# Moving four side steps in the schedule of a one-core hybrid decoder layer

## What is computed

```python
u = rmsnorm(h, g_pre)
p = u @ w_in                       # 4096 x (12*1024 + 8)
log_f = log_sigmoid(f_logit + b_forget)            # the 8 extra columns, one per FoX head
o_fox = forgetting_attention(fq, fk, fv, log_f) * silu(fgate)
o_sb  = stick_breaking_attention(sq, sk, sv) * silu(sgate)
o_ssm = s5_mixer(su, ...) * silu(ssm_gate)         # complex diagonal scan, gelu, GLU
o_lru = rglru_mixer(lx, ...) * silu(lru_gate)      # conv4, block gates, scan
out = h + rmsnorm(concatenate([o_fox, o_sb, o_ssm, o_lru]) @ w_out, g_post)
```

## Time and profile before

| | |
|---|---|
| Median of 3 runs | 1551.7 us (1551.67 to 1552.07) |
| The profiled execution | 1551.9 us |
| Its span, first to last instruction | 1550.0 us |
| Granted TensorE clock, mean | 0.997 |
| PE matmul busy | 1525.6 us (98%), 7090 recorded |
| DVE busy | 927.1 us (60%) |
| ACT busy | 858.8 us (55%) |
| POOL busy | 86.6 us (6%) |
| Mean transfer rate | 188 GB/s |

### The profile page before, as it was taken

The page is one execution under the profiler, slowest core; times in us unless marked ns, Lnnn a source line. Parts: engine busy times, 40 slices in busy tenths (PEclk is TensorE's granted clock), DMA queues, the critical chain, the costliest instruction groups (busy, mean ns, idle before and its releaser), DMA issues.

```text
span 1550.0 us, 22156 instructions
## 1 busy us (share of the span) xinstructions
PE 1525.6 (98%) x7090; PEld 1254.7 (81%) x7090; DVE 927.1 (60%) x1154; ACT 858.8 (55%) x1158; POOL 86.6 (6%) x130
## 2 busy tenths in 40 slices
PE   8999999999999999999999999999999999999996
PEld 7888887778877788888878888888888888888885
DVE  6544478899888895454554544455566444444445
ACT  6644476666776656566554445556666443444442
POOL 0000010111211110000000000000000000000000
PEclk9999999999999999999999999999999999999999
DMA  8466656665665665565655555555556866666675
GB/s 303 136 198 190 188 167 186 181 198 172 183 186 179 194 192 177 181 198 172 194 162 165 175 163 166 171 179 176 164 172 201 276 193 196 193 191 192 194 232 179
DMA packets 86104, 291.26 MB, mean 188 GB/s; under 512 B 9904, under 2 KB 13232, under 8 KB 86064
## 3 DMA queue, kind: packets, MB, share of 16 engines
q1 hardware_dynamic: 77328, 276.86, 59.3%
q10 hardware_dynamic: 8736, 13.89, 2.7%
HBM read 286.51 MB, written 4.19 MB: 188 GB/s over the span
## 4 chain that ended last, share of the span: by engine, by line
PE 90%; DVE 4%; issue 2%; ACT 2%; DMA 1%; SPq 0%; DVEq 0%; POOL 0%; ACTq 0%; POOLq 0%
PE main L261 28%; PE main L263 28%; PE main L262 27%; PE side L392 2%; DMA w_raw<-in_wall 1%; PE main L286 1%; DVE vals L1062 1%; PE side L354 1%; PE side L343 0%; DVE w_lo L843 0%; PE side L318 0%; ACT w_hi L519 0%; PE side L386 0%; PE side L409 0%; DVE vals L1068 0%
## 5 line engine op out<-in xcount | busy, mean ns | idle before, releaser
L843 DVE TENSOR_TENSOR w_lo<-w_raw,w_hi 128x1024 fp32r<-128x1024 f32 x512 | 634.6, 1243 | 581.6 <-ACT w_hi L519 580.9
L519 ACT ACTIVATE w_hi<-w_raw 128x1024 fp32r<-128x1024 f32 x512 | 540.5, 1058 | 604.9 <-PE main L263 586.1
L261 PE MATMUL main<-w_hi,acts 128*128 128x512 f32 x2032 | 803.3, 395 | 3.9 <-ACT cross L528 2.5
L263 PE MATMUL main<-w_hi,acts 128*128 128x512 f32 x2032 | 792.9, 390 | 0.0
L262 PE MATMUL main<-w_lo,acts 128*128 128x512 f32 x2032 | 791.9, 390 | 0.0
L261 PEld LDWEIGHTS main<-w_hi,acts 128*128 128x128 f32 x2032 | 382.2, 188 | 89.6 <-ACT cross L528 5.2
L263 PEld LDWEIGHTS main<-w_hi,acts 128*128 128x128 f32 x2032 | 381.9, 188 | 81.0
L262 PEld LDWEIGHTS main<-w_lo,acts 128*128 128x128 f32 x2032 | 382.4, 188 | 76.4
L1341 POOL TENSOR_TENSOR scr<-scr 128x256 f32<-128x256 f32 x32 | 31.3, 977 | 491.5 <-ACT scr L611 491.5
L1062 DVE TENSOR_TENSOR_SCAN vals<-small,vals 128x256 f32<-128x256 f32 x64 | 40.9, 680 | 0.0
L1364 POOL COPY scr<-br 128x256 f32 x16 | 12.3, 769 | 372.7 <-DVE head_sel L1169 309.9
(11 more groups left out here) (247 smaller groups left out, 744.8 us busy)
## 6 DMA issues: line engine op xcount, KB each, us to landing
w_raw<-in_wall SPq DMA_DIRECT2D x512, 512.0 KB, 3.6
br<-in_x SPq DMA_DIRECT2D x16, 256.0 KB, 7.9
scr<-in_wglu ACTq DMA_DIRECT2D x8, 512.0 KB, 3.5
out<-br SPq DMA_DIRECT2D x7, 512.0 KB, 2.7
br<-in_gpost ACTq DMA_DIRECT2D x8, 256.0 KB, 4.6
vals<-in_x ACTq DMA_DIRECT2D x8, 256.0 KB, 5.0
scr<-in_x ACTq DMA_DIRECT2D x8, 256.0 KB, 4.2
scr<-in_bt ACTq DMA_DIRECT2D x32, 32.0 KB, 2.6
```

Source lines behind the costliest of these rows:

```text
L261: pe.matmul(main[:, bank0 + a, :], u_h, wh, start=(k == 0), stop=False)
L263: mm = pe.matmul(main[:, bank0 + a, :], u_l, wh, start=False, stop=(k == NK - 1))
L519: act.activation(w_hi[:, c % RING, :], w_raw[:, c % RING, :], ACT.Copy).then_inc(hi_ready, 1)
L843: dve.tensor_tensor(w_lo[:, c % RING, :], w_raw[:, c % RING, :], w_hi[:, c % RING, :].bitcast(F32), ALU.subtract).then_inc(lo_ready, 1)
```

## The change

The forget chain moves into block 1: the token rows ahead of chunk 3, bias and clearing at DVE's step 4, Abs, Exp and Ln at ACT's step 5, `logf` at DVE's step 7, the running sums ahead of chunk 9, the split at steps 10 and 11. It uses banks 2 and 1 of `side`, and `dec_rows` gets a buffer of its own. For this ACT's and DVE's loops over the source blocks get their first turn written out. `C_AT` becomes 15. A Silu of one column is added to ACT's step 14 in the gate blocks. The stick-breaking transposes and their copy move from +5 to +6.

```diff
+        dec_rows = sb("dec_rows", [96, T], BF16)[:, :]
...
-        C_AT = CH - 2
+        C_AT = CH - 1
...
             def src_block(i):
+                def token_logits():
+                    pe.wait_ge(fl_dve, 1)
+                    for a in range(TT):
+                        mm = pe.matmul(side[:, 2, a * FT:(a + 1) * FT], fl_rows[0:2 * FT, a * P:(a + 1) * P],
+                                       fl_sel, start=True, stop=True)
+                    mm.then_inc(fl_mm, 1)
+
+                def forget_sums():
+                    pe.wait_ge(lf_ready, 3)
+                    pe.matmul(side[0:ROWS, 1, 0:P], logf[:, 0, :], upto[:, :], start=True, stop=True)
...
                 for c in range(CH):
                     if c == T_AT:
                         turn_rows(i - 1, i - 1)
+                    if c == 3 and isinstance(i, int):
+                        token_logits()
+                    if c == 9 and isinstance(i, int):
+                        forget_sums()
                     chunk_in(i, c)
...
-            pe.wait_ge(side_free, FT + 1)
-            for a in range(TT):
-                mm = pe.matmul(side[:, 3, a * FT:(a + 1) * FT], fl_rows[0:2 * FT, a * P:(a + 1) * P], fl_sel,
...
-                    if c == 1 and isinstance(i, int):
-                        pe.wait_ge(lf_ready, 3)
-                        pe.matmul(side[0:ROWS, 3, 0:P], logf[:, 0, :], upto[:, :], start=True, stop=True)
...
-                        if c == SB_AT[a] + 5:
+                        if c == SB_AT[a] + 6:
                             pe.wait_ge(at_exp, i * 2 + (2 * FT + a + 1))
                             transposes(h)
...
-            with act.Fori(1, B_QK - B_SRC) as i:
+            def src_block(i):
                 for c in range(CH):
                     high(i, c + LEAD)
...
+                    if c == 5 and isinstance(i, int):
+                        act.wait_ge(fl_dve, 3)
+                        act.activation(fl_e, fl_z, ACT.Abs).then_inc(fl_act, 1)
+                        act.wait_ge(fl_act, 2)
+                        act.activation(fl_e, fl_e, ACT.Exp, scale=-1.0).then_inc(fl_act, 1)
+                        act.wait_ge(fl_act, 3)
+                        act.activation(fl_e, fl_e, ACT.Ln, bias=1.0).then_inc(fl_act, 1)
+                    if c == 10 and isinstance(i, int):
+                        act.wait_ge(dec_mm, 1)
+                        act.activation(dec_rows, side[0:ROWS, 1, 0:T], ACT.Copy, scale=-1.0).then_inc(dec_neg, 1)
...
+                    if c == CH - 2:
+                        act.activation(small[:, 146:147], later[:, 0:1], ACT.Silu)
                     if c == CH - 1:
                         take_gate(i + B_G1)
...
-                        if c == SB_AT[a] + 5:
+                        if c == SB_AT[a] + 6:
                             copy_weights(h)
+                    if c == CH - 2:
+                        act.activation(small[:, 146:147], later[:, 0:1], ACT.Silu)
                     if c == CH - 1:
                         take_gate(i + B_G2)
...
+            def src_block(i):
                 for c in range(CH):
                     low(i, c + LEAD)
+                    if c == 4 and isinstance(i, int):
+                        forget_values()
+                    if c == 7 and isinstance(i, int):
+                        log_forgets()
+                    if c == 11 and isinstance(i, int):
+                        decay_rows()
+
+            src_block(1)
+            with dve.Fori(2, B_QK - B_SRC) as i:
+                src_block(i)
...
-            dve.wait_ge(fl_act, 4)
-            dve.wait_ge(fl_dve, 2)
-            dve.wait_ge(glu_applied, 1)
-            dve.memset(logf, 0.0).then_inc(fl_dve, 1)
...
```

More of the change, by code:

```diff
@@ L111, in hybrid_trunk @@
         ROWS = 96
-        logf = scr[:, 3072:3072 + TT * ROWS].rearrange("p (a n) -> p a n", a=TT)
+        logf = scr[:, 4912:4912 + TT * ROWS].rearrange("p (a n) -> p a n", a=TT)
+        dec_mid = scr[0:ROWS, 768:896].bitcast(BF16)
+        dec_r1, dec_r2 = scr[0:ROWS, 2816:3072], scr[0:ROWS, 3072:3328]
         steps_t = scr[:, 3328:3328 + T]
@@ L323, in src_block @@
             def src_block(i):
+                def token_logits():
[7 more added lines that the diff above has]
+                    pe.matmul(side[0:ROWS, 1, 0:P], logf[:, 0, :], upto[:, :], start=True, stop=True)
+                    pe.matmul(side[0:ROWS, 1, P:T], logf[:, 0, :], later[:, 0:P], start=True, stop=False)
+                    pe.matmul(side[0:ROWS, 1, P:T], logf[:, 1, :], upto[:, :], start=False,
+                              stop=True).then_inc(dec_mm, 1)
                 for c in range(CH):
@@ L419, in fox_block @@
                         turn_rows(i + (B_G1 - 1), i + (T_GATE - 1))
-                    if c == 1 and isinstance(i, int):
-                        pe.wait_ge(lf_ready, 3)
-                        pe.matmul(side[0:ROWS, 3, 0:P], logf[:, 0, :], upto[:, :], start=True, stop=True)
-                        pe.matmul(side[0:ROWS, 3, P:T], logf[:, 0, :], later[:, 0:P], start=True, stop=False)
-                        pe.matmul(side[0:ROWS, 3, P:T], logf[:, 1, :], upto[:, :], start=False,
-                                  stop=True).then_inc(dec_mm, 1)
                     for a in range(2):
@@ L730, in fox_block @@
                     high(i + B_G1, c + LEAD)
-                    if c == 2 and isinstance(i, int):
-                        act.wait_ge(dec_mm, 1)
-                        act.activation(dec_rows, side[0:ROWS, 3, 0:T], ACT.Copy, scale=-1.0).then_inc(dec_neg, 1)
                     for a in range(2):
@@ L1013, in _ @@
             dve.tensor_tensor(fl_rows[0:2 * FT, :], side[0:2 * FT, 3, 0:T], fl_cross[0:2 * FT, :],
-                              ALU.add).then_inc(side_free, 1)
+                              ALU.add).then_inc(fl_dve, 1)
             def take_s5(f):
@@ L1025, in _, with forget_values, log_forgets, decay_rows @@
             take_s5(0)
-            with dve.Fori(1, B_QK - B_SRC) as i:
+            def forget_values():
+                dve.wait_ge(fl_mm, 2)
+                for a in range(TT):
+                    dve.scalar_tensor_tensor(fl_z[:, a, :], side[:, 2, a * FT:(a + 1) * FT], rstd[:, a:a + 1],
+                                             col("b_forget")[:, a * FT:(a + 1) * FT], ALU.mult,
+                                             ALU.add).then_inc(fl_dve, 1)
+                dve.memset(logf, 0.0).then_inc(fl_dve, 1)
+            def log_forgets():
+                dve.wait_ge(fl_act, 4)
+                dve.wait_ge(fl_dve, 4)
+                for n in range(3):
+                    dve.scalar_tensor_tensor(logf[:, :, 32 * n:32 * n + FT], fl_z, 0.0, fl_e, ALU.min,
+                                             ALU.subtract).then_inc(lf_ready, 1)
+            def decay_rows():
+                dve.wait_ge(dec_neg, 1)
+                dve.scalar_tensor_tensor(dec_r1, side[0:ROWS, 1, 0:T], -1.0, dec_rows, ALU.mult,
+                                         ALU.subtract).then_inc(dec_dve, 1)
+                dve.wait_ge(dec_dve, 1)
+                dve.tensor_scalar(dec_mid, dec_r1, 1.0, None, ALU.mult).then_inc(dec_dve, 1)
+                dve.wait_ge(dec_dve, 2)
+                dve.tensor_tensor(dec_r2, dec_r1, dec_mid, ALU.subtract).then_inc(dec_dve, 1)
+                dve.tensor_scalar(dec_rows[32:64, :], dec_mid[32:64, :], 1.0, None, ALU.mult).then_inc(dec_dve, 1)
+                dve.wait_ge(dec_dve, 3)
+                dve.tensor_scalar(dec_rows[64:96, :], dec_r2[64:96, :], 1.0, None, ALU.mult).then_inc(side_free, 1)
+            def src_block(i):
                 for c in range(CH):
                     low(i, c + LEAD)
+                    if c == 4 and isinstance(i, int):
[4 more added lines that the diff above has]
+                        decay_rows()
+            src_block(1)
+            with dve.Fori(2, B_QK - B_SRC) as i:
+                src_block(i)
             dve.wait_ge(t_free, FT // JB)
@@ L1085, in _ @@
             s5_block(B_V - B_QK - 1)
[L1088 to L1093, removed]
             dve.wait_ge(t_free, B_QK)
```

15 lines of the change are left out of this document (2 added, 13 removed).

## The result

| | before | changed |
|---|---|---|
| Median | 1551.68 us (6 runs, 1549.90 to 1552.19) | 1542.55 us (6 runs, 1542.33 to 1542.86) |
| Profiled execution, its span | 1551.9, 1550.0 us | 1542.66, 1540.9 us |
| PE matmul busy | 98% | 99% |

The ratio is 0.9943, with a 95% interval of 0.993 to 0.9956: 9.1 us or 0.6% less. The forecast was 1541.9 us (1540.6 to 1545.8).

The account below looks back on a forecast made before the run. PE, busy 98% of the span, was taken to bound the kernel. The terms 3.81 + 3.73 + 0.92 + 1.3 = 9.8 us took the profiled 1551.9 to 1542.1, and the median 0.2 lower to 1541.9 us (range 1540.6 to 1545.8).

Parts of the forecast that it names:

- 1, the forget chain: Block 16's running sums: 2.18 us of wait and 1.63 us of lower clock go, 3.81 us; block 1 costs zero.
- 2, the Silu table: Table load moves from the evacuation to step 14; four block boundaries stop losing, 3.73 us; the others give nothing.
- 3, the transposes: Block 23's late transposes, one chunk later, lose their wait for ACT's weights: 0.92 us.
- It is even; I take no wait: Block 23: copy back and PE's reach of the values both about 1159.8; no wait taken, 0.3 us kept for the range.
- 4, the S5 outputs: Outputs one chunk later: 0.90 us in blocks 5 to 10, 0.4 in block 4 after a 0.8 us wait; together 1.3.
- No S5 block showed a fall of the clock: Rival: late handover at s5_inputs idles PE about 2 us and drags the clock down in seven blocks; 1570 us, chance 2%.
- block 16 found no other wait: Rival: another wait replaces the removed one in block 16 and the clock falls again; 3.8 us stay, 1545.7, chance 6%.
- no table load stayed at the evacuation: Rival: the table load stays at the evacuation or delays it from step 14; up to 3.7 us stay, 1545.6, chance 5%.

Follow-up runs that it names:

- take_first: Changed kernel, DVE taking S5 outputs ahead of step 15's low, ACT copying stick-breaking weights back ahead of the mix copies; 1541.36 us.
- the last repeat: The changed kernel with the stick-breaking transposes and their copy back at +5, run once more for one profiled execution; 1543.3 us.
- outputs_at_14: The changed kernel with C_AT, the chunk of the S5 outputs, back at 14; 1543.52 us.
- transposes_at_5: The changed kernel with the stick-breaking transposes and their copy back at +5; 1543.47 us.

## Why the prediction was right

**1, the forget chain.** Right in mechanism and in size against the execution that it was made from: 28.64 us became 24.72, which is 3.92 us, and 3.8 without the 0.11 us of a gap between side and main matmuls that moved away with the sums. What the step did not say is that 1.63 us of it were the cost of one execution: one repeat of the kernel before had the same idle and no fall of the clock. Against such runs the chain is worth 2.2 us. That the six runs of the kernel before had a median of 1551.68, on the side of the fall, helped the size of the gain to come out as forecast, and that is luck; the time of the changed kernel does not depend on it, because its profile has no such fall.

**2, the Silu table.** 1.07 + 0.77 + 0.76 + 1.09 = 3.69 us measured, 3.73 forecast. The step held in the tightest place with 0.21 us to spare, and at the other boundaries nothing changed, as taken.

**3, the transposes.** The wait of 0.92 us went. "It is even; I take no wait" was the term that was off: PE's value product waited. The PE timeline shows it, and beneath it ACT's copy, which ends at 1152.26:

```profile
1151.91 0.39 PE L264 MATMUL main<-w_hi,acts 128*128 128x512 f32 x1
1152.32 0.70 PE L422 MATMUL side<-scr 128*128 128x256 f32 x2
```

```profile
1151.79 0.47 ACT L734 ACTIVATE scr<-side 128x384 f32<-128x384 f32 x1
```

With the copy put first (`take_first`) the chunk takes 2.84 us and the same two matmuls 0.59:

```profile
1151.13 0.59 PE L422 MATMUL side<-scr 128*128 128x256 f32 x2
```

The chunk is 0.18 us longer than that, and the product starts slower by 0.1: some 0.3 us, the bound that the range had kept. The net gain is 0.6 us.

**4, the S5 outputs.** Block 4 went from 47.13 us (204.90 to 252.03) to 46.71, a gain of 0.4 as forecast, with a wait of 0.7 us where 0.8 was expected. Block 5 went from 46.05 to 45.92, 0.13 us where 0.15 was taken, and its five successors lost no more (47.0 us from one block's inputs to the next's, 47.1 before). Together that is 1.2 us where 1.3 was forecast. DVE's row of block 4 confirms the order of the sum: four `low`, then the outputs.

```profile
247.32 5.17 DVE L858 TENSOR_TENSOR w_lo<-w_raw,w_hi 128x1024 fp32r<-128x1024 f32 x4
252.41 0.47 DVE L1136 SCALAR_TENSOR_TENSOR br<-br,pars,side 128x256 f32 x1
```

**The rest.** Forecast 9.8 us, measured 9.1 in the spans and in the medians. The transposes account for 0.3 of the difference, the S5 outputs for 0.1, and about 0.2 were lost between the gate products of blocks 13 and 14 (24.85 us instead of 24.72, and gate products of 4.23 us instead of 4.13), at the late transfer shown with the last repeat. The list of waits does not name it, and the profiles of `outputs_at_14`, `transposes_at_5` and `take_first`, with the same steps there, do not have it: like the fall of the clock, it is the cost of one execution. Another 0.2 us lie behind the last matmul: 12.3 us from its start to the end before (1537.67 to 1550.0), 12.5 after (1528.36 to 1540.9). Their cause stays open.

**The rivals.** No S5 block showed a fall of the clock, block 16 found no other wait, and no table load stayed at the evacuation.

## What to carry to other kernels

On an engine that is busy 98% of the time, find the losses by comparing stretches of equal work, not by the list of waits; each stretch that exceeds its twin names a wait, and the sum of the excesses forecast this change within 0.7 of 9.8 us. For every step that is moved, work out who waits next and by how much it fits: the running sums one chunk later gave 1.5 us back at the scores, and the outputs one chunk later gave 0.7 back at the inputs until the taking was put ahead of `low`. Before a term goes into a sum, ask whether it is there in each execution: a profile shows one.

## What the hardware did that I had not expected

- After the idle of 2.0 us at the sums the granted clock fell to its lower level (1.2 of 2.4 GHz) in four of five profiled executions, each time at a cost of about 1.6 us, and did not in the fifth. After 3.2 us there it fell (one profile, 1.3 us), after 1.6 us it did not (one profile). An idle of 2.1 us in block 0 was not followed by a fall, nor were the idles of 0.4 to 1.5 us in any profile here.
- The Trainium skill, "ScalarE: Activation LUTs", section "Table sets: the hidden batching unit", says that Ln and then Exp can share one set with a single load. The runs here show it otherwise: Exp and Ln of the forget chain each had a load of 1.28 us, before (at 793.50 and 795.02) and after the move (at 86.98 and 88.50, the second in the row of block 1 above), and in block 23 of the changed kernel the Exp that follows Ln, with only copies between them, had another:

```profile
1140.00 0.53 ACT L785 ACTIVATE scr<-scr 128x384 f32<-128x384 f32 x1
...
1143.67 1.28 ACT L788 ACT_TABLE_LOAD   x1
```

- The length of block 0, up to the logit matmuls, differs by 0.6 us between executions of one kernel (62.3 to 62.9 us), which is as much as some of the effects looked for here.
- A transfer of 128 KB that was issued right behind one of 512 KB took 5.9 to 7.1 us in 39 of 42 cases and 7.3 to 7.6 us in the other three, and each of these three held PE by 0.2 to 0.5 us, though only one of them shows as a wait for a transfer.
